# The last channel chunk of a causal convolution: from diagonal products on TensorE to scaled rows on ScalarE and sums on GpSimd

## The chip, the cores and the metric

The kernel runs on one NeuronCore of one Trainium2 chip. Five engines run their own instruction streams and meet only at semaphores: TensorE (PE; its weight loads are PEld), VectorE (DVE), ScalarE (ACT), GpSimd (POOL) and SyncE (SP), which issues nearly all DMAs. The metric is the time of one execution on the device, in microseconds (us), lower is better. The time of a kernel is the median of its runs.

## The reference, cut to what matters

Two transformer blocks follow each other. The change lies in the first one, for 512 tokens of width 1024: a projection feeds a sliding-window attention and a depthwise causal convolution of width 31 over 512 channels, and both results go through one output product. Everything is float32.

```python
def conformer_conv(u, conv_dw, conv_dw_b, conv_ln_g, conv_ln_b, w_conv_pw):
    a, gate = jnp.split(u, 2, axis=-1)
    h = a * jax.nn.sigmoid(gate)
    h = lax.conv_general_dilated(h, conv_dw[:, None, :], window_strides=(1,),
        padding=[(CONV_WIDTH - 1, 0)], feature_group_count=D_CONV, ...) + conv_dw_b
    h = jax.nn.silu(layer_norm(h, conv_ln_g, conv_ln_b))
    return h @ w_conv_pw

def sliding_window_attention(q, k, v, attn_sinks, rel_bias):
    # blocks of 128 queries; each sees its own and the previous 128 keys
    s = einsum(qb, kb) * scale + bias[bucket]          # masked outside the band
    m = max(max(s), sink); p = exp(s - m)
    p = p / (sum(p) + exp(sink - m))
    return einsum(p, vb)

hn = rms_norm(h, mix_pre_g); proj = hn @ w_in
mixed = concatenate([attn_out, conv_out], -1) @ w_out
h = h + rms_norm(mixed, mix_post_g)
```

Then come a gated feed-forward layer and the second block (another attention with a top-k choice of keys, and a mixture over 16384 experts). They are the same in both kernels.

## The kernel before

**Tiling.** The convolution holds channels on the 128 partitions, in four chunks c = 0 to 3 (CC = 4), and tokens along the row (T = 512). `hpad[:, c, :]` is a chunk's gated input with 30 zeros ahead of it. One tap w of a chunk is `cacc += taps[w] * hpad[:, c, w:w+512]`, a 128x512 scalar_tensor_tensor on VectorE (line 1786) that reads two tiles of SBUF. 31 taps make a chunk. Attention works in four blocks b of 128 queries, with 8 heads.

**Weights.** Every large product runs in three float32r passes (high and low halves), so a weight unit goes through three steps: SyncE loads it into `wraw` (three buffers), ScalarE rounds it into `WH` (line 1191, `cast_to`), and the low half `WL` is a subtraction of two SBUF tiles, on GpSimd (line 1140) or, for units 4 to 13 (`BESIDE_TAPS`) and a few others, on VectorE (line 2297). Units 8 to 13 are the keys, the values and the four query tiles; units 14 and 15 are the first of the output product.

**Order.** All orders are written out by hand, one program per engine, and nothing reorders them. VectorE goes through the taps of chunks 0, 1 and 2, with a `low` of a unit at every sixth tap; the second half of chunk 2's taps (16) is spread over the four attention blocks. On ScalarE the projections' results are copied out in the order keys, vT, q0, v, q1, q2, q3. Ahead of each copy stands `cast_to` of a unit two ahead. Each of these waits in order: an instruction that waits holds all that stand behind it.

**Chunk 3 is computed differently.** ScalarE makes diagonal matrices `tap_diag` (identity times tap, 128x128, line 1292), a few behind each copy, by `diags_plan`. TensorE multiplies them with the shifted rows of `hpad` and sums the 31 products in PSUM, in four groups `("cv", g)` (line 657), one group at the head of each attention block. VectorE adds a group's sum into `cacc[:, 3]` (lines 1852 and 1855).

**Attention.** PE: scores (line 624), transposes of the probabilities (line 636), weighted values (line 645). DVE: `logits(b)` (scale and bias, maximum; lines 1821 to 1829), `normalise(b)` (1835 to 1838), four taps of chunk 2, the group's sum, and `low(b-1)`, the low half of the block's output (1845), which frees a PSUM bank. ACT: exponentials (1302), diagonals, copies of the transposed probabilities (1311), the block's output (1315). PSUM has eight banks, taken in turn: the tile that takes a bank waits until the one eight places earlier is read. For block 1's last transpose that one is block 0's output, which `low(0)` frees.

**After attention** `conv_tail` takes the mean over the four chunks (line 682), for which every chunk must be done, and then the output product begins.

## Time and profile before

| | us |
|---|---|
| median of 3 runs | 2167.96 |
| lowest and highest run | 2166.16, 2172.48 |
| span of the profiled execution (first to last instruction) | 2161.6 |
| from the gated input of chunk 3 to the first scores | 81.75 to 104.11 |
| attention stage: first scores to the mean of the convolution | 104.11 to 165.55 |

The stage that the change touches is the short stretch from 76 to 170 us of the span. The rest of the kernel is bound by TensorE. Times in the rows count from the span's start. In a timeline row the first number is the start, the second how long the instruction (or the xN merged ones) took, and in brackets stands the idle time of the engine before it and what ended it. "took" includes the time in which an instruction has been started but can't proceed. The median of the runs is 6.4 us above the profiled span; the profiled execution has no other time of its own.

### The profile page before, as it was taken

Reading aid. Unit: us, or ns where it says so; the run is one execution under the profiler, and the core shown is the slowest. Engines: PE = TensorE matmul, PEld = TensorE weight load, DVE = VectorE, ACT = ScalarE, POOL = GpSimd, SP = SyncE. Lnnn points to the kernel's source line nnn. Section 1 sums busy time; section 2 is a strip of 40 time slices with the busy share of each in tenths; the row PEclk is TensorE's granted clock in tenths of the full one; section 3 lists DMA queues with packets and bytes.
Section 4 is the critical chain, followed back from the end, with each engine's and each line's share of the span. In section 5 each row is a group of like instructions: output and inputs, shape, how many; then the busy total and the mean of one; then the engine's idle time right before and its main releaser. Section 6 shows DMA issues by size and latency. Waiting matters only on the chain.

```text
span 2161.6 us, 29125 instructions
## 1 busy us (share of the span) xinstructions
PE 2121.7 (98%) x10648; PEld 1837.8 (85%) x10648; DVE 1442.4 (67%) x2713; ACT 858.3 (40%) x1306; POOL 1038.6 (48%) x573
## 2 busy tenths in 40 slices
PE   8989999999999999999999999999999999999999
PEld 7857888888877877899999999999998888888887
DVE  5973411110054995369998777787867999999987
ACT  4354522232264454253334444444433333333332
POOL 1203244443423333435566888888863444444342
PEclk9999999999999999999999999999999999999999
DMA  4202344444442222334347899998899999999996
GB/s 177 82 27 62 104 117 127 117 119 115 117 118 74 86 71 77 117 106 121 112 147 207 242 267 321 284 315 249 261 309 318 388 388 371 373 375 377 369 359 251
DMA packets 240489, 444.14 MB, mean 205 GB/s; under 512 B 102459, under 2 KB 152028, under 8 KB 240220
## 3 DMA queue, kind: packets, MB, share of 16 engines
q1 hardware_dynamic: 152060, 299.07, 41.8%
q0 software_dynamic: 55488, 134.83, 19.3%
q10 hardware_dynamic: 32800, 8.39, 1.8%
q8 instruction: 85, 1.39, 0.3%
q14 instruction: 56, 0.46, 0.1%
HBM read 397.71 MB, written 44.50 MB: 205 GB/s over the span
## 4 chain that ended last, share of the span: by engine, by line
PE 69%; POOL 13%; DVE 8%; issue 4%; DMA 3%; ACT 2%; SPq 0%; DVEq 0%; ACTq 0%; POOLq 0%
PE bank L469 22%; PE bank L473 22%; PE bank L472 22%; POOL gate_matrices L1151 9%; POOL y L1160 4%; DMA y<-in_peer_u_rows,gidx 3%; DVE m L1979 1%; PE bank L923 1%; DVE xn L1980 1%; DVE WL L2297 1%; PE bank L645 1%; DMA wraw<-in_peer_u 1%; ACT sc L1302 1%; DVE y L2308 0%; DVE hots L2329 0%
## 5 line engine op out<-in xcount | busy, mean ns | idle before, releaser
L1140 POOL TENSOR_TENSOR WL<-wraw,WH 128x1024 fp32r<-128x1024 f32 x171 | 435.9, 2552 | 723.5 <-ACT WH L1191 723.5
L1191 ACT ACTIVATE WH<-wraw 128x1024 fp32r<-128x1024 f32 x411 | 435.0, 1060 | 627.4 <-PE bank L469 393.6
L469 PE MATMUL bank<-XH,WH 128*128 128x384 f32 (+2 forms) x1864 | 668.8, 359 | 12.6 <-DVE WL L2297 7.8
L473 PE MATMUL bank<-XH,WL 128*128 128x384 f32 (+2 forms) x1864 | 657.8, 353 | 0.0
L472 PE MATMUL bank<-XL,WH 128*128 128x384 f32 (+2 forms) x1864 | 657.6, 353 | 0.0
L469 PEld LDWEIGHTS bank<-XH,WH 128*128 128x128 f32 x1864 | 351.4, 189 | 46.3 <-issue 12.9
L472 PEld LDWEIGHTS bank<-XL,WH 128*128 128x128 f32 x1864 | 351.6, 189 | 29.0 <-issue 0.7
L473 PEld LDWEIGHTS bank<-XH,WL 128*128 128x128 f32 x1864 | 351.1, 188 | 28.7
L2297 DVE TENSOR_TENSOR WL<-wraw,WH 128x1024 fp32r<-128x1024 f32 x240 | 293.0, 1222 | 57.6 <-ACT WH L1191 51.8
L469 PE MATMUL bank<-WH,GH 128*128 128x512 f32 x768 | 298.9, 389 | 1.6 <-issue 1.6
L473 PE MATMUL bank<-WH,GL 128*128 128x512 f32 x768 | 298.8, 389 | 0.0
L472 PE MATMUL bank<-WL,GH 128*128 128x512 f32 x768 | 298.8, 389 | 0.0
L1160 POOL DMA_INDIRECT y<-in_peer_v,gidx x128 | 185.2, 1447 | 220.7 <-DVE hN L2316 203.0
L1151 POOL DMA_INDIRECT gate_matrices<-scat_gate,scat_at x128 | 243.7, 1904 | 40.9 <-issue 38.4
L2308 DVE CUSTOM_DVE_ANT_0 y<-y,x_nat 128x1024 f32<-128x1024 f32 x128 | 156.0, 1223 | 108.6 <-DMA y<-in_peer_u_rows,gidx 103.4
L1160 POOL DMA_INDIRECT y<-in_peer_u_rows,gidx x128 | 169.3, 1323 | 106.1 <-DVE gdot L2308 77.0
L469 PEld LDWEIGHTS bank<-WH,GH 128*128 128x128 f32 x768 | 144.1, 188 | 32.3 <-issue 2.3
L473 PEld LDWEIGHTS bank<-WH,GL 128*128 128x128 f32 x768 | 144.1, 188 | 29.9
L472 PEld LDWEIGHTS bank<-WL,GH 128*128 128x128 f32 x768 | 144.2, 188 | 29.8
L2316 DVE SCALAR_TENSOR_TENSOR hN<-y,gdot,hN 128x1024 f32<-128x1024 f32 x128 | 163.9, 1280 | 3.6 <-DMA y<-in_peer_v,gidx 0.6
L1589 ACT ACTIVATE ac<-bank 128x384 f32<-128x384 f32 x122 | 59.8, 490 | 239.0 <-PE bank L473 223.6
L1904 DVE TENSOR_TENSOR y<-bank,y 128x512 f32<-128x512 f32 x22 | 15.2, 692 | 208.2 <-PE bank L473 208.2
(313 smaller groups left out, 2561.8 us busy)
## 6 DMA issues: line engine op xcount, KB each, us to landing
wraw<-in_peer_u SPq DMA_DIRECT2D x128, 512.0 KB
wraw<-in_peer_v SPq DMA_DIRECT2D x128, 512.0 KB
activations<-ac SPq DMA_DIRECT2D x122, 192.0 KB
ar<-activations SPq DMA_DIRECT2D x122, 192.0 KB
gr<-gate_matrices SPq DMA_DIRECT2D x124, 128.0 KB
wraw<-in_w_gate SPq DMA_DIRECT2D x22, 512.0 KB
wraw<-in_w_up SPq DMA_DIRECT2D x22, 512.0 KB
wraw<-in_w_down SPq DMA_DIRECT2D x22, 512.0 KB
```

Source lines behind the costliest of these rows:

```text
L469: mm = pe.matmul(out, wh, xh, start=first, stop=False)
L472: pe.matmul(out, wh, xl, start=False, stop=False)
L473: return pe.matmul(out, wl, xh, start=False, stop=last)
L645: mm = pe.matmul(out[half, (h % 4) * P:(h % 4 + 1) * P], v1[:, b - 1 + kt, half], pT1[:, h, kt, :], start=kt == kts[0], stop=kt == 1)
L1140: pool.tensor_tensor(WL[:, u % NW, 0:m], wraw[:, u % NR, 0:m], WH[:, u % NW, 0:m].bitcast(F32), ALU.subtract).then_inc(s("w_lo"), 1)
L1151: pool.indirect_dma_start(out=gate_cells[:, :], out_offset=bass.IndirectOffsetOnAxis(ap=scat_at[:, k:k + 1], axis=0), in_=scat_gate[:, k:k ...
L1160: pool.indirect_dma_start(out=gathered[:, row % NGATHER, :], out_offset=None, in_=(u_rows if row < HS else v_rows)[:, :], in_offset=bass.I ...
L1191: act.activation(WH[:, u % NW, 0:k * n], wraw[:, u % NR, 0:k * n], ACT.Copy).then_inc(s("w_hi"), 1)
L1589: act.activation(ac[:, x % NAC, :] if x < SENT else kept[:, x - SENT, :], src[:, 0:TD], ACT.Gelu_apprx_tanh).then_inc(frees(("a", x)), 1)
L2297: dve.tensor_tensor(WL[:, u % NW, 0:k * n], wraw[:, u % NR, 0:k * n], WH[:, u % NW, 0:k * n].bitcast(F32), ALU.subtract).then_inc(made, 1)
L2308: dve.tensor_tensor_reduce(out=at, in0=at, in1=x_nat[:, :], scale=1.0, scalar=0.0, op0=ALU.mult, op1=ALU.add, accum_out=gdot[:, row:row + ...
L2316: dve.scalar_tensor_tensor(out=hN[:, NTD, :], in0=at, scalar=gdot[:, row - HS:row - HS + 1], in1=hN[:, NTD, :], op0=ALU.mult, op1=ALU.add) ...
```

## The change

Chunk 3's taps leave TensorE and PSUM. ScalarE writes `taps[w] * hpad[:, 3, w:w+512]` (128x512) into one of four slots `tap_scaled`, the bias going into the first. GpSimd adds the products up in `cacc[:, 3]`, 30 additions of 128x512, each waiting for the product (`tap_scaled`) and for the addition before (`tap_added`). The product w waits for addition w-4, whose slot it takes (and for the first addition, where w is 4 or 5). `scaled_plan` says how many products follow each copy: 0, 4, 4, 0, 4, 4, 4 in the projections, and 6 and 5 in attention blocks 0 and 1.

Four orders change with it:

- GpSimd does all the additions ahead of the low half of unit 14.
- VectorE makes the gated input of chunk 3 some six taps earlier and has no group sums.
- TensorE has no group of tap products at a block's head, and `scores(b + 2)` now stands behind `weighted_values(b)`.
- ScalarE does the exponentials of block b+1 ahead of the products and copies of block b.

The first place is ScalarE, from the cast of unit 11 to the copy of q1. `WH` is a cast, `xn` and `cln` are the tiles that hold diagonals or products. Before:

```order
L1191 ACTIVATE WH<-wraw 128x1024
L1280 ACTIVATE vT<-bank 128x512
L1292 ACTIVATE xn<-ident,taps 128x128 x3
L1191 ACTIVATE WH<-wraw 128x1024
L1280 ACTIVATE q<-bank 128x512
L1292 ACTIVATE xn<-ident,taps 128x128 x2
L1191 ACTIVATE WH<-wraw 128x1024
L1280 ACTIVATE v<-bank 128x512
L1292 ACTIVATE cln<-ident,taps 128x128 x2
L1280 ACTIVATE q<-bank 128x512
```

After:

```order
L1189 ACTIVATE WH<-wraw 128x1024
L1278 ACTIVATE vT<-bank 128x512
L1291 ACTIVATE xn<-hpad,vec,taps 128x512
L1291 ACTIVATE xn<-hpad,taps 128x512
L1291 ACTIVATE cln<-hpad,taps 128x512 x2
L1189 ACTIVATE WH<-wraw 128x1024
L1278 ACTIVATE q<-bank 128x512
L1291 ACTIVATE xn<-hpad,taps 128x512 x2
L1291 ACTIVATE cln<-hpad,taps 128x512 x2
L1189 ACTIVATE WH<-wraw 128x1024
L1278 ACTIVATE v<-bank 128x512
L1278 ACTIVATE q<-bank 128x512
```

Behind the copies of vT and of each q there now stand four 128x512 products in place of two or three 128x128 diagonals; the casts keep their places behind them, and from the fifth product on each waits for GpSimd.

The second place is TensorE at the head of attention: `kk,q` are scores (the row of 128x128 is block 0, the next ones blocks 1 and 2), `hpad,xn` and `hpad,cln` tap products, `ident,sc` transposes, `pT,v` weighted values. Before:

```order
L624 MATMUL bank<-kk,q 128x128 x8
L624 MATMUL bank<-kk,q 128x256 x8
L657 MATMUL bank<-hpad,xn 128x512 x8
L624 MATMUL bank<-kk,q 128x256 x8
L636 MATMUL bank<-ident,sc 128x128 x8
L645 MATMUL bank<-pT,v 64x128 x8
L657 MATMUL bank<-hpad,cln 128x512 x8
```

After:

```order
L623 MATMUL bank<-kk,q 128x128 x8
L623 MATMUL bank<-kk,q 128x256 x8
L635 MATMUL bank<-ident,sc 128x128 x8
L644 MATMUL bank<-pT,v 64x128 x8
L623 MATMUL bank<-kk,q 128x256 x8
L635 MATMUL bank<-ident,sc 128x128 x16
L644 MATMUL bank<-pT,v 64x128 x16
```

The tap products are gone, and block 2's scores moved from ahead of block 0's transposes to behind its weighted values.

```diff
--- before.py
+++ after.py
@@ -307,9 +307,8 @@
             oneh = sb("oneh", [BUCKETS + 1, SKEW], F32, sc)
             cln = sb("cln", [P, 2, T], F32, sc)
 
-        tap_diag = [tile[:, a, m * P:(m + 1) * P] for tile in (xn, cln) for a in range(2) for m in range(4)]
-        diags_plan = [3, 3, 2, 2, 2, 2, 2, 8, 7]
-        TAP_GROUPS = [(0, 8), (8, 16), (16, 24), (24, TAPS)]
+        tap_scaled = [tile[:, a, :] for tile in (xn, cln) for a in range(2)]
+        scaled_plan = [0, 4, 4, 0, 4, 4, 4, 6, 5]
         brow = sc1[:, :, :, :].rearrange("p a h n -> p (a h n)")[:, 0:NH * SKEW].rearrange("p (h n) -> p h n", h=NH)
         skew_dram = nc.dram_tensor("skew_rows", (P, NH, SKEW), F32).ap()
 
@@ -646,26 +645,13 @@
                                        pT1[:, h, kt, :], start=kt == kts[0], stop=kt == 1)
                 full(mm, "o", b)
 
-            def last_chunk_taps(g):
-
-                w0, w1 = TAP_GROUPS[g]
-                out = take("cv", g)
-                for w in range(w0, w1):
-                    pe.wait_ge(s("diags_made"), w + 1)
-                    if w == 0:
-                        wait_read(pe, ("ca", CC - 1))
-                    mm = pe.matmul(out[:, :], tap_diag[w % len(tap_diag)], hpad[:, CC - 1, w:w + T], start=w == w0,
-                                   stop=w == w1 - 1)
-                full(mm, "cv", g)
-
             def attention():
                 scores(0)
                 scores(1)
                 for b in range(NT):
-                    last_chunk_taps(b)
+                    weighted_values(b)
                     if b + 2 < NT:
                         scores(b + 2)
-                    weighted_values(b)
 
             def mixed(i):
 
@@ -678,7 +664,7 @@
                     if c < CC - 1:
                         pe.wait_ge(s("conv_done"), c + 1)
                     else:
-                        wait_read(pe, ("cv", NT - 1))
+                        pe.wait_ge(s("tap_added"), TAPS - 1)
                     mm = pe.matmul(out[:, :], ones[:, :], cacc[:, c, :], start=c == 0, stop=c == CC - 1)
                 full(mm, "cmean", 0)
                 for b in range(NT):
@@ -1063,7 +1049,7 @@
                 if u == unit_at[("ci", 0)] + 2:
                     second_inputs()
                 if u == unit_at[("wo", 0, 2)]:
-                    wait_full(sp, ("cv", NT - 1))
+                    sp.wait_ge(s("tap_added"), TAPS - 1)
                     sp.dma_start(gain_row, A["mix_post_row"].partition_broadcast(P)).then_inc(s("post_row_landed"), 16)
                 if u >= unit_at[("wg", 4)] and (u - unit_at[("wg", 4)]) % 4 == 0 and u < unit_at[("wg", 4)] + 4 * (NEXP // ZBLOCKS):
                     if u == unit_at[("wg", 4)]:
@@ -1122,9 +1108,21 @@
                       allow_small_or_imprecise_dtypes=True).then_inc(s("own_row_made"), 1)
             pool.memset(zeros[:, :], 0.0).then_inc(s("zeros_made"), 1)
 
+            def last_chunk():
+
+                at = cacc[:, CC - 1, :]
+                for w in range(1, TAPS):
+                    pool.wait_ge(s("tap_scaled"), w + 1)
+                    if w > 1:
+                        pool.wait_ge(s("tap_added"), w - 1)
+                    pool.tensor_tensor(at, tap_scaled[0] if w == 1 else at, tap_scaled[w % len(tap_scaled)],
+                                       ALU.add).then_inc(s("tap_added"), 1)
+
             for u, (k, n, _) in enumerate(units[:LOW_BY_DVE]):
                 if u in BESIDE_TAPS or u in NORM_LOWS:
                     continue
+                if u == BESIDE_TAPS.stop:
+                    last_chunk()
                 if u == unit_at[("u2", 1)]:
                     pool.wait_ge(s("wsr_landed"), 16)
                     pool.affine_select(out=wsr[:, :, :], in_=wsr[:, :, :], compare_op=ALU.is_ge, fill=0.0, base=0,
@@ -1278,23 +1276,25 @@
                     cast_to(("v", 0) if key == ("vT", 0) else ("q", 1) if key == ("v", 0) else key)
                     src = wait_full(act, key)
                     act.activation(dst, src[:, :], ACT.Copy).then_inc(frees(key), 1)
-                    last_chunk_diags()
-
-            diags, stages = [0], iter(diags_plan)
-
-            def last_chunk_diags():
-
-                for w in range(diags[0], diags[0] + next(stages, 0)):
-                    if w >= len(tap_diag):
-                        g = next(n for n, (w0, w1) in enumerate(TAP_GROUPS) if w0 <= w - len(tap_diag) < w1)
-                        wait_full(act, ("cv", g))
-                    at = w * CC + CC - 1
-                    act.activation(tap_diag[w % len(tap_diag)], ident[:, :], ACT.Copy,
-                                   scale=taps[:, at:at + 1]).then_inc(s("diags_made"), 1)
-                    diags[0] = w + 1
+                    last_chunk_products()
+
+            scaled, stages = [0], iter(scaled_plan)
+
+            def last_chunk_products():
+
+                c = CC - 1
+                for w in range(scaled[0], scaled[0] + next(stages, 0)):
+                    if w == 0:
+                        wait_read(act, ("ca", c))
+                    if w >= len(tap_scaled):
+                        act.wait_ge(s("tap_added"), max(w - len(tap_scaled), 1))
+                    act.activation(tap_scaled[w % len(tap_scaled)], hpad[:, c, w:w + T], ACT.Identity,
+                                   scale=taps[:, w * CC + c:w * CC + c + 1],
+                                   bias=vcol("dw_b", c) if w == 0 else 0.0).then_inc(s("tap_scaled"), 1)
+                    scaled[0] = w + 1
 
             def attention():
-                for b in range(NT):
+                def exps(b):
                     w = P if b == 0 else 2 * P
                     st = st1[:, b % 2]
                     act.wait_ge(s("sink_gap"), b + 1)
@@ -1302,7 +1302,12 @@
                         act.activation(sc1[:, b % 2, h, 0:w], sc1[:, b % 2, h, 0:w], ACT.Exp, bias=st[:, 1, h:h + 1],
                                        accum_out=st[:, 2, h:h + 1])
                     act.activation(st[:, 4, :], st[:, 3, :], ACT.Exp).then_inc(s("exps"), 1)
-                    last_chunk_diags()
+
+                exps(0)
+                for b in range(NT):
+                    if b + 1 < NT:
+                        exps(b + 1)
+                    last_chunk_products()
                     for i in range(NH // 2):
                         src = wait_full(act, ("pT", b, i))
                         kt0 = 1 if b == 0 else 0
@@ -1799,7 +1804,7 @@
                         tap(c, w)
                         if w - alone < alone:
                             tap(c + 1, w - alone)
-                        if c == CC - 3 and w == alone:
+                        if c == 0 and w == TAPS - 3:
                             gated(CC - 1)
                 for u in beside:
                     low(u, s("w_beside"))
@@ -1845,16 +1850,6 @@
                     dve.tensor_tensor(XL[:, 0:4, to], src[:, :].rearrange("p (c q) -> p c q", c=4),
                                       XH[:, 0:4, to].bitcast(F32), ALU.subtract).then_inc(frees(("o", b)), 1)
 
-                def last_chunk(g):
-                    src = wait_full(dve, ("cv", g))
-                    at = cacc[:, CC - 1, :]
-                    if g == 0:
-                        done = dve.tensor_scalar(at, src[:, :], vcol("dw_b", CC - 1), None, ALU.add)
-                    else:
-                        wait_read(dve, ("cv", g - 1))
-                        done = dve.tensor_tensor(at, at, src[:, :], ALU.add)
-                    done.then_inc(frees(("cv", g)), 1)
-
                 logits(0)
                 for b in range(NT):
                     if b + 1 < NT:
@@ -1862,7 +1857,6 @@
                     normalise(b)
                     for w in taps_left[b * len(taps_left) // NT:(b + 1) * len(taps_left) // NT]:
                         tap(w)
-                    last_chunk(b)
                     if b:
                         low(b - 1)
                 low(NT - 1)
```

## Rows read from the trace of the kernel before

**Rows 1.** The page: busy shares, and shares of the chain of waits.
```profile
PE 2121.7 (98%) x10648; PEld 1837.8 (85%) x10648; DVE 1442.4 (67%) x2713; ACT 858.3 (40%) x1306; POOL 1038.6 (48%) x573
PE 69%; POOL 13%; DVE 8%; issue 4%; DMA 3%; ACT 2%; SPq 0%; DVEq 0%; ACTq 0%; POOLq 0%
```

**Rows 2.** Windows: PE, PEld, DVE, ACT, POOL busy us (count), PEclk, DMA share, GB/s.
```profile
76.00:104.00 28.00, 27.23 (x122) 22.20 (x121) 27.89 (x41) 12.61 (x27) 9.41 (x1) 1.00 0.23 75
104.11:165.55 61.44, 55.12 (x294) 35.41 (x294) 44.12 (x65) 30.91 (x105) 4.34 (x2) 0.97 0.08 26
```

**Rows 3.** Timeline, VectorE, end of the convolution: no row has idle time before it.
```profile
81.75 0.68 DVE L1770 TENSOR_TENSOR hpad<-bank,sg 128x512 f32<-128x512 f32 x1
82.35 3.40 DVE L1786 SCALAR_TENSOR_TENSOR cacc<-hpad,taps,cacc 128x512 f32<-128x512 f32 x5
...
86.80 4.06 DVE L1786 SCALAR_TENSOR_TENSOR cacc<-hpad,taps,cacc 128x512 f32<-128x512 f32 x6
90.77 1.22 DVE L2297 TENSOR_TENSOR WL<-wraw,WH 128x1024 fp32r<-128x1024 f32 x1
91.91 12.01 DVE L1786 SCALAR_TENSOR_TENSOR cacc<-hpad,taps,cacc 128x512 f32<-128x512 f32 x18
```

**Rows 4.** Timeline, GpSimd: its low half of unit 14, beside that chain.
```profile
94.59 11.54 POOL L1140 TENSOR_TENSOR WL<-wraw,WH 128x1024 fp32r<-128x1024 f32 x1 [63.86 <-ACT WH L1191]
```

**Rows 5.** Groups by form, GpSimd, whole span: busy us, mean ns of one.
```profile
L1140 POOL TENSOR_TENSOR WL<-wraw,WH 128x1024 fp32r<-128x1024 f32 x170 | 434.6, 2559 | 723.5 <-ACT WH L1191 723.5
...
L1140 POOL TENSOR_TENSOR WL<-wraw,WH 128x544 fp32r<-128x544 f32 x1 | 1.4, 1358 | 0.0
```

**Rows 6.** Timeline, ScalarE: the last cast and copy of the projections.
```profile
98.90 1.05 ACT L1191 ACTIVATE WH<-wraw 128x1024 fp32r<-128x1024 f32 x1
103.26 0.60 ACT L1280 ACTIVATE q<-bank 128x512 f32<-128x512 f32 x1 [3.31 <-PE bank L473]
```

**Rows 7.** Timeline, VectorE, first block of attention.
```profile
105.38 1.29 DVE L1821 SCALAR_TENSOR_TENSOR sc<-bank,biasT 128x512 f32<-128x512 f32 x2 [1.46 <-PE bank L624]
...
107.96 0.51 DVE L1827 TENSOR_TENSOR st<-st,sinkb 128x8 f32<-128x8 f32 x1
...
108.66 2.48 DVE L1821 SCALAR_TENSOR_TENSOR sc<-bank,biasT 128x512 f32<-128x512 f32 x4
111.17 2.29 DVE L1826 TENSOR_REDUCE st<-sc 128x8 f32<-128x2048 f32 x1
...
115.42 3.11 DVE L1786 SCALAR_TENSOR_TENSOR cacc<-hpad,taps,cacc 128x512 f32<-128x512 f32 x4
```

**Rows 8.** Timeline, a later stage: a GpSimd pass, and VectorE's third of four rows.
```profile
634.55 2.43 POOL L1140 TENSOR_TENSOR WL<-wraw,WH 128x1024 fp32r<-128x1024 f32 x1 [3.83 <-ACT WH L1191]
634.63 2.63 DVE L1949 SCALAR_TENSOR_TENSOR ck<-ck,st,gkv 128x256 f32<-128x256 f32 x1
```

**Rows 9.** Windows, the tap products' matmuls (line 657) alone in the attention stage.
```profile
104.11:165.55 61.44, 28.16 (x62) 11.61 (x62) 0.97 0.08 26
```

**Rows 10.** Groups by form, 76 to 190 us: ScalarE and VectorE in attention.
```profile
L1302 ACT ACTIVATE sc<-sc,st 128x256 f32<-128x256 f32 x24 | 11.8, 495 | 0.0
...
L1838 DVE TENSOR_TENSOR sc<-sc,st 128x2048 f32<-128x2048 f32 x3 | 6.9, 2291 | 0.1
...
L1311 ACT ACTIVATE pT<-bank 128x512 f32<-128x512 f32 x12 | 6.3, 601 | 8.6 <-PE bank L636 8.6
...
L1202 ACT ACTIVATE sq<-cacc 128x512 f32<-128x512 f32 x4 | 2.5, 631 | 5.7 <-DVE cacc L1875 4.5 <-PE bank L502 1.2
```

**Rows 11.** Timeline, TensorE: weighted values of blocks 0 and 1.
```profile
120.55 2.71 PE L645 MATMUL bank<-pT,v 128*64 128x128 f32 x16 [0.86 <-DVE sc L1821]
...
136.90 3.33 PE L645 MATMUL bank<-pT,v 128*64 128x128 f32 x32 [0.86 <-DVE sc L1821]
```

**Rows 12.** Windows ahead of and over block 0's weighted values (columns as in rows 2).
```profile
118.00:120.80 2.80, 0.69 (x4) 0.46 (x5) 2.19 (x4) 0.38 (x1) 0.00 (x0) 0.99 0.00 0
120.80:124.20 3.40, 3.40 (x18) 2.56 (x17) 3.37 (x4) 0.91 (x3) 0.00 (x0) 0.50 0.02 7
```

## The prediction, made before the changed kernel was run

> **What bounds the kernel now.** I read first the page, then windows over the two stages that the change touches, then the timelines of each engine in them, last the groups for durations. The page shows TensorE busy for 98% of the span and as most of the chain of waits [rows 1]. That is a mean, and it hides the stretch at issue. From 76 to 104 us VectorE is busy for 27.9 of 28 us, TensorE for 27.2, and ScalarE and GpSimd have room [rows 2]; TensorE sets the pace there, with VectorE close behind. From the first scores at 104.1 to the mean of the convolution at 165.55, which is 61.4 us, no engine is full: TensorE 55.1, VectorE 44.1, ScalarE 30.9 [rows 2]. Half of TensorE's part are the tap products, 28.2 us in 62 passes [rows 9]. The chain goes logits, maximum, exponentials, normalise, transposes, copies, weighted values, and the tap products lie mostly beside the exponentials. So their 28 us are not for the taking.
>
> **What the change adds.** ScalarE: 31 products of 128x512. A square of that shape takes 0.63 us [rows 10]; back to back I take 0.54, since a cast of twice the width takes 1.05 [rows 6]. GpSimd: 30 additions of 128x512 with two SBUF operands. It has 2.56 us for 1024 columns and 1.36 for 544 [rows 5], so 1.28 for 512 by the slope. Bounds are 1.0 and 1.4; with the wait on its own last result I take 1.31, thus 39 us in one serial chain.
>
> **The step that decides: two engines, one way into SBUF.** GpSimd's low half of unit 14 started at 94.59 and took 11.54 us, where 2.56 is usual [rows 4, 5]. Beside it VectorE ran taps without a gap until 103.9 [rows 3]; 103.9 + 2.2 is 106.1, the end of GpSimd's row. So GpSimd did nothing while the taps ran, though it had asked for 13 boundaries between them. The other way round, a 128x8 operation took 0.51 us while GpSimd's second pass was under way [rows 7]. The new additions read two SBUF tiles as that pass did, and stand beside the same taps.
>
> The Trainium skill, page "SBUF — State Buffer", part "Who interferes with whom", says that a VectorE instruction with two SBUF inputs and a GpSimd instruction that reads SBUF exclude each other for a whole instruction, and that whichever issues first goes first. The exclusion agrees with [rows 4]. First come, first served does not, since GpSimd then had its turn at 95.3; a later place agrees with it [rows 8]. That reading is the first rival below.
>
> **Projections, step by step.** The gated input of chunk 3 is written some 5 us earlier than at 81.75 [rows 3], which costs VectorE nothing. Products 0 to 3 come behind the copy of vT (81.0), so the first addition can start at 82.7. VectorE has then begun its gapless row. ScalarE goes on to the copy of q0 and blocks at product 4 (87.0), which waits for addition 1. Behind it in ScalarE's queue stands the cast of unit 13, for whose low half VectorE comes by at 90.8 [rows 3]. VectorE stops there, and that frees the way. Additions 1 to 3 end at 92.2, 93.5 and 94.8; product 7 and the cast follow until 96.3; VectorE, behind addition 5, does the low half from 97.4 to 98.5. TensorE wants unit 13 at 97.8, one copy of 5.4 us ahead of 103.26 [rows 6], so it loses 0.8.
>
> VectorE now has its 18 last taps, 12.0 us [rows 3], and shuts GpSimd out until 110.5. ScalarE blocks at product 10, which waits for addition 6. Behind it stand the copies of q2 and q3. Product 15, the last ahead of the copy of q3, waits for addition 11. Additions 6 to 11 take 6 x 1.31 = 7.9, until 118.4; the product, a cast (0.95) and the copy (0.60) give the first scores at 120.5 in place of 104.1: **+16.4 us**. Who waits is TensorE, with nothing else to do.
>
> **Attention, step by step, at full clock.** Scores at 120.5. Logits 0 took 3.3 us [rows 7] and now wait twice behind an addition, 2.4: 126.4. Logits 1 are 2.5 + 2.3 and 0.3 of small ones [rows 7]: 131.5. ScalarE has exponentials 1 (8 x 0.49 [rows 10]) until 135.7 and then six products, of which the last waits for addition 21. Additions 20 and 21 wait for VectorE's normalise and four taps (3.1 [rows 7]) and end at 139.0. The copies of transposed probabilities stand behind that, so block 0's values end at 141.6, and only then come scores 2: 21.1 us for this block. Block 1: logits 2 until 147.4, normalise (2.3 [rows 10] and 0.3) until 150.0, four taps and the low half, which frees a bank for the last transpose, until 153.8. ScalarE meanwhile has exponentials 2 and five products until 154.9. Four copies at 0.5 [rows 10] and the values (3.3 [rows 11]) bring scores 3 at 158.9: 17.3. Block 2: logits, normalise, taps, low half, last transpose, values: 175.1, 16.2. Block 3 needs only transposes and values, its exponentials having been made ahead: 180.3, 5.3. The sum is 59.9 against 61.4: **-1.5**. What the missing 28 us of tap products give, the later scores take back: logits(b + 2) can't start before block b is through. VectorE's four group sums (0.7 each) count in this. The last addition is at 159, well ahead of the mean, and the low half of unit 14 at 162 is early enough; the loads of units 17 and 18, which wait for low halves, come 50 us later than before and are still first needed past 185.
>
> **The clock.** After 2.8 us with TensorE busy for 0.69 the granted clock was 0.50 for 3.4 us [rows 12], the lower level of 1.2 GHz against 2.4. Block 0's 16 passes took 2.71 us there, 0.169 each, against 32 in 3.33, 0.104 each, at full clock [rows 11]: 1.6 times. In the new order TensorE idles for 16 us ahead of the first scores and for some 6 us in each block. On the path it carries about 13 us of transposes, values and scores in the sum above. At 0.6 of that, all at half clock, the price is 8; the other bound is nothing. I take 7, since the drop shown came after a far shorter pause: **+7**.
>
> Sum: +16.4 - 1.5 + 7 = 21.9. The profiled span of 2161.6 becomes 2183.5. The median of the runs is 6.4 above the span, so I forecast **2190 us**. With additions of 1.0 us it is 3 less, with 1.4 it is 2 more, and the clock gives 2182 to 2191.
>
> **Rivals.** *The two engines take turns (20%).* At one place GpSimd asked while a VectorE instruction ran, and the next one, though started without a gap, took 2.63 us behind it [rows 8]. Then from 82.7 on VectorE's 21 us of work in the convolution and about 19 additions of 1.31 share the way, and logits 0 start near 129 instead of 105.4 (+24); attention, with fewer additions left, gives back 3; the clock adds 7: 2196. Against it stand the same instructions at the same place [rows 4].
>
> *They hardly disturb each other (17%).* If ScalarE's products came early enough and additions slipped in beside taps, scores would start at 104.1, and attention without waits behind additions would take about 57 us: -4, or 2164 at full clock; with spells of half clock 2164 to 2172. It needs that the 9 us of standstill [rows 4] be something else than VectorE's taps. I split it into 11% faster and 6% the same. 0.3%, or 6.5 us, is about what a measurement of this kernel can tell from no change.
>
> *The standstill is real but shorter (10%).* VectorE stops once more, or the copies of q2 and q3 get ahead: half of the 16.4, so +8 to +14: 2176 to 2182. *No change in effect* is no case: every engine's order differs.
>
> **How the numbers follow.** The forecast has 50%, taking turns 20%, the shorter standstill 10%, no disturbance 17%, and 3% something slower still. Slower by over 0.3% is thus 83%, faster 11%, the same 6%. The range reaches from 2172, which leaves out the faster rival, to 2204, which takes in taking turns with the longest additions.
>
> **What the new profile would show.** Right: additions on GpSimd of many microseconds beside the taps, the first at about 83 that ends past 91 and one of over 10 us that ends past 110; the first scores at 118 to 123; TensorE idle ahead of them; the low clock in attention; 58 to 68 us from the scores to the mean. Wrong in the main step: additions of 1.3 us all along and scores near 104, or taps that each take 2 us. Wrong in the second: an attention stage under 55 us. The stretch behind 190 us of the span should be the same, only shifted.

## The result, and the profile after

The changed kernel takes 2185.41 us (median of 4 runs, 2182.96 to 2188.93) against 2167.82 us for the kernel before (4 runs beside it). The ratio is 1.0076 with a 95% interval of 1.0054 to 1.0097: slower by 17.6 us. The prediction said 2190 and a range of 2172 to 2204. The size came out near; the way to it did not, and that is what the runs are about.

The profiled execution has a span of 2181.0 us against 2161.6. Its busy shares and its chain of waits, as in [rows 1]:

```profile
PE 2105.0 (97%) x10586; PEld 1836.0 (84%) x10586; DVE 1457.4 (67%) x2709; ACT 866.3 (40%) x1306; POOL 1077.8 (49%) x603
PE 76%; DVE 9%; POOL 7%; DMA 3%; issue 3%; ACT 2%; SPq 0%; DVEq 0%; ACTq 0%; POOLq 0%
```

TensorE has 62 matmuls fewer, and VectorE is busy for 15 us longer with four instructions fewer. Something makes VectorE's instructions longer. Since executions differ by some us ahead of the change already (a spell of half clock that comes early or late), I count all stages from ScalarE's copy of vT. It started at 81.02 in the trace of before and at 78.02 here.

| us, from the copy of vT | before | after |
|---|---|---|
| to the first scores | 23.09 | 33.56 |
| first scores to first logits | 1.27 | 5.62 |
| first logits to the mean of the convolution | 60.17 | 63.82 |
| sum: copy of vT to the mean | 84.53 | 103.00 |
| from the mean to the end | 1996.1 | 2000.0 |

The sum says where the time went: 18.5 us between the copy of vT and the mean, nearly all of the difference. What lies behind the mean varied between 1991.7 and 2011.6 us over the profiled executions of all kernels here, though its instructions are the same, and nothing is read from that.

VectorE in the projections, where [rows 3] had five taps in 3.40 us, six in 4.06 and eighteen in 12.01 (timeline: start, us, engine, line, operation, output<-inputs, count):

```profile
80.13 8.61 DVE L1791 SCALAR_TENSOR_TENSOR cacc<-hpad,taps,cacc 128x512 f32<-128x512 f32 x5
88.66 2.30 DVE L2291 TENSOR_TENSOR WL<-wraw,WH 128x1024 fp32r<-128x1024 f32 x1
90.88 10.22 DVE L1791 SCALAR_TENSOR_TENSOR cacc<-hpad,taps,cacc 128x512 f32<-128x512 f32 x6
101.02 2.28 DVE L2291 TENSOR_TENSOR WL<-wraw,WH 128x1024 fp32r<-128x1024 f32 x1
103.22 14.05 DVE L1791 SCALAR_TENSOR_TENSOR cacc<-hpad,taps,cacc 128x512 f32<-128x512 f32 x18
```

And GpSimd beside it, the additions of the new sum:

```profile
80.00 1.36 POOL L1118 TENSOR_TENSOR cacc<-xn 128x512 f32<-128x512 f32 x1 [48.98 <-ACT xn L1291]
81.50 3.27 POOL L1118 TENSOR_TENSOR cacc<-cacc,cln 128x512 f32<-128x512 f32 x2
...
102.36 3.76 POOL L1118 TENSOR_TENSOR cacc<-cacc,cln 128x512 f32<-128x512 f32 x2
112.01 7.79 POOL L1118 TENSOR_TENSOR cacc<-cacc,xn 128x512 f32<-128x512 f32 x2 [5.89 <-ACT xn L1291]
```

Six taps in 10.22 us are 1.70 each, where 0.67 was usual. Two additions in 3.27 (with the 0.14 between them) are 1.56 each. One pair, a tap and an addition, takes 1.70 us: 0.4 of the tap's and 1.3 of the addition's. So the two engines take turns, one instruction each, from 80 us until the fifteenth addition ends at 106.1. Then GpSimd has no product for 5.9 us, and its sixteenth addition, asked for at 112.01, is held up for 5 us until VectorE's last tap is over at 117.3. That one row looks like [rows 4]; the fifteen ahead of it look like [rows 8].

What TensorE and ScalarE make of it (in brackets the idle time ahead, and what ended it):

```profile
91.10 0.47 PE L468 MATMUL bank<-XH,WH 128*128 128x512 f32 x1 [1.75 <-DVE WL L2291]
103.44 0.77 PE L468 MATMUL bank<-XH,WH 128*128 128x512 f32 x1 [6.63 <-DVE WL L2291]
```

```profile
104.31 1.06 ACT L1189 ACTIVATE WH<-wraw 128x1024 fp32r<-128x1024 f32 x1 [4.42 <-PE bank L468]
110.73 0.60 ACT L1278 ACTIVATE q<-bank 128x512 f32<-128x512 f32 x1 [5.36 <-PE bank L472]
```

TensorE waits 1.75 and 6.63 us for VectorE's low halves of two weight units, which stand behind eleven slow taps; the rest of the 10.5 us is the product for q3, part of it at half clock. ScalarE's products are not what anybody waits for: they find an addition missing once in this stretch, for 0.33 us.

In attention TensorE's rows read like this (compare block 0's values in [rows 11], 2.71 and 3.33, and the clock in [rows 12]):

```profile
111.57 3.41 PE L623 MATMUL bank<-kk,q 64*128 64x128 f32 x32 [0.88 <-ACT q L1278]
128.12 1.97 PE L635 MATMUL bank<-ident,sc 128*128 128x128 f32 x8 [13.13 <-DVE sc L1843]
135.20 2.85 PE L644 MATMUL bank<-pT,v 128*64 128x128 f32 x16 [5.12 <-ACT pT L1316]
137.98 3.46 PE L623 MATMUL bank<-kk,q 64*128 64x256 f32 x16
148.17 2.82 PE L635 MATMUL bank<-ident,sc 128*128 128x128 f32 x12 [6.73 <-DVE sc L1843]
...
156.66 2.10 PE L623 MATMUL bank<-kk,q 64*128 64x256 f32 x16
165.79 2.82 PE L635 MATMUL bank<-ident,sc 128*128 128x128 f32 x12 [7.04 <-DVE sc L1843]
...
170.46 5.47 PE L644 MATMUL bank<-pT,v 128*64 128x128 f32 x32
```

And VectorE's logits of blocks 2 and 3, with the time it stood idle for the scores that now come late:

```profile
140.09 2.58 DVE L1826 SCALAR_TENSOR_TENSOR sc<-bank,biasT 128x512 f32<-128x512 f32 x4 [9.01 <-PE bank L623]
...
157.82 2.48 DVE L1826 SCALAR_TENSOR_TENSOR sc<-bank,biasT 128x512 f32<-128x512 f32 x4 [5.07 <-PE bank L623]
```

Three things can hide in these 18.5 us: additions in the way of VectorE, scores that come after the values instead of ahead, and TensorE at half clock. The windows over both stages show the last (busy us and count of PE, PEld, DVE, ACT, POOL, then PEclk):

```profile
94.00:104.00 10.00, 3.37 (x14) 2.50 (x13) 10.00 (x7) 3.04 (x5) 9.28 (x6) 0.79 0.00 0
111.57:181.02 69.45, 34.81 (x233) 30.50 (x233) 48.95 (x70) 35.17 (x103) 28.99 (x17) 0.68 0.07 24
```

### The profile page after: what moved, and what is told of

It reads as the page before. It is cut to its first block, busy times and chain, and to the rows that moved or that the text cites. A ratio compares the mean times of both kernels' runs of the same rounds, so it can differ in the third digit from the quotient of the medians.

```text
span 2181.0 us, 29049 instructions
## 1 busy us (share of the span) xinstructions
PE 2105.0 (97%) x10586; PEld 1836.0 (84%) x10586; DVE 1457.4 (67%) x2709; ACT 866.3 (40%) x1306; POOL 1077.8 (49%) x603
## 4 chain that ended last, share of the span: by engine, by line
PE 76%; DVE 9%; POOL 7%; DMA 3%; issue 3%; ACT 2%; SPq 0%; DVEq 0%; ACTq 0%; POOLq 0%
PE bank L468 24%; PE bank L472 24%; PE bank L471 23%; POOL gate_matrices L1149 5%; DVE cacc L1791 2%; POOL y L1158 2%; PE bank L937 1%; DMA y<-in_peer_u_rows,gidx 1%; DVE m L1973 1%; PE bank L644 1%; DMA wraw<-in_peer_u 1%; PE bank L909 1%; DVE WL L2291 1%; DVE xn L1974 1%; DVE sc L1826 0%
## 5 line engine op out<-in xcount | busy, mean ns | idle before, releaser
L1138 POOL TENSOR_TENSOR WL<-wraw,WH 128x1024 fp32r<-128x1024 f32 x171 | 425.5, 2491 | 624.6 <-ACT WH L1189 624.6
L1898 DVE TENSOR_TENSOR y<-bank,y 128x512 f32<-128x512 f32 x22 | 15.2, 692 | 208.2 <-PE bank L472 208.2
```

Source lines behind the costliest of these rows:

```text
L1138: pool.tensor_tensor(WL[:, u % NW, 0:m], wraw[:, u % NR, 0:m], WH[:, u % NW, 0:m].bitcast(F32), ALU.subtract).then_inc(s("w_lo"), 1)
```

## The experiments

In the kernels' names below, "early scores" means that TensorE makes the scores of block b+2 ahead of the values of block b. Stage times are from one profiled execution each. The stage from the copy of vT to the first scores came out between 23.08 and 23.10 us in seven kernels, so a stage can be read to about 0.1 us where nothing disturbs it. Where additions disturb it, it can't. Four of the kernels are the same up to the first scores (the change, early scores, the fill at one addition, fillers on TensorE), and their stage took 33.56, 33.07, 33.06 and 31.92 us. The run with the fill is nearly a second execution of the whole changed kernel, and it has 100.5 us from the copy of vT to the mean where the first had 103.0. So differences against the 103.0 are good to some 2.5 us, not to tenths.

### Additions that read nothing

```diff
-                    pool.tensor_tensor(at, tap_scaled[0] if w == 1 else at, tap_scaled[w % len(tap_scaled)],
-                                       ALU.add).then_inc(s("tap_added"), 1)
+                    pool.memset(at, 0.0).then_inc(s("tap_filled"), 1)
+                    pool.wait_ge(s("tap_filled"), w)
+                    pool.memset(at, 0.5).then_inc(s("tap_added"), 1)
```

> The changed kernel with each of GpSimd's 30 additions replaced by two fills of the accumulator, which write SBUF and read none of it; the sum of the last chunk is left out. Theory (VectorE's taps and GpSimd's additions exclude each other because both read SBUF): the taps from 80 us on take 0.7 to 0.8 us each and stand without gaps as in the kernel before, and from the copy of vT to the first scores it takes 23 to 25 us (23.1 before, 33.6 after). Rival (ScalarE's products, each of which waits for an addition, and the copies queued behind them cost the time, whatever the additions do): 30 us or more at fills of the same length, and taps of 0.75 us with TensorE waiting for ScalarE's copies. Rival (any GpSimd work on SBUF disturbs, writes too): taps of 1.5 us or more again.

Timeline of VectorE and of GpSimd:

```profile
92.07 12.01 DVE L1792 SCALAR_TENSOR_TENSOR cacc<-hpad,taps,cacc 128x512 f32<-128x512 f32 x18
```

```profile
93.65 0.53 POOL L1118 MEMSET cacc<- 128x512 f32 x1
94.23 0.53 POOL L1120 MEMSET cacc<- 128x512 f32 x1
```

The taps are back at 12.01 us for eighteen, to the hundredth what [rows 3] had, and vT to scores takes 23.10. From vT to the mean it takes 85.3 us, against 103.0. A pair of fills has 1.23 us from start to start and is chained as the additions were (1.41 in the undisturbed pairs), so the chain of products and waits was still there, nearly as long. GpSimd that only writes leaves the taps as they are; GpSimd *reading* SBUF costs 17.7 us, or 15.2 against the 100.5 of the second execution. The rival, that ScalarE blocks behind its products, falls.

### Additions of half the length

```diff
+                    if w == 1:
+                        pool.memset(at, 0.0).then_inc(s("acc_zeroed"), 1)
+                        pool.wait_ge(s("acc_zeroed"), 1)
-                    pool.tensor_tensor(at, tap_scaled[0] if w == 1 else at, tap_scaled[w % len(tap_scaled)],
+                    pool.tensor_tensor(at[:, 0:T // 2], tap_scaled[0][:, 0:T // 2] if w == 1 else at[:, 0:T // 2],
...
```

> The changed kernel with each addition over 256 of the 512 columns (the other half of the last chunk's sum is left out, the accumulator is cleared first). Theory (turns: each tap waits for one addition): additions of 0.65 to 0.75 us in place of 1.3, taps at a spacing of 1.2 to 1.3 us in place of 1.8, from the copy of vT to the first scores 27 to 30 us (33.6 after), and the attention stage 2 to 4 us shorter than 69.5. Rival (starvation behind the gapless taps sets the time): unchanged within 2 us, since the wait doesn't depend on how long an addition is. Rival (the additions are off the path in attention): attention stays at 69.5 within 1 us.

```profile
88.72 6.48 DVE L1794 SCALAR_TENSOR_TENSOR cacc<-hpad,taps,cacc 128x512 f32<-128x512 f32 x6
95.13 1.76 DVE L2294 TENSOR_TENSOR WL<-wraw,WH 128x1024 fp32r<-128x1024 f32 x1
```

Additions took 0.73 us alone, and a disturbed tap 1.21 to 1.23: the turns hold. But the stage to the first scores went all the way back, 23.09, where 27 to 30 were expected. Six taps in 6.48 us let the low half end at 96.9, and TensorE wants it at about 97.9. The delay is no sum of slow taps; it is what is left of it beyond VectorE's reserve ahead of a low half. What the additions still cost shows one step later, 9.3 us from the first scores to the first logits, since VectorE must finish its taps first. The attention stage came to 70.4, no shorter than 69.5, as the second rival had it; from the first logits it is 61.2 against 63.8.

### Products and additions in attention only

```diff
-        scaled_plan = [0, 4, 4, 0, 4, 4, 4, 6, 5]
+        scaled_plan = [0, 0, 0, 0, 0, 0, 0, 9, 9, 8, 5]
```

> The changed kernel with no products and additions during the projections: the stages of ScalarE make 9, 9, 8 and 5 products in the four blocks of attention. Theory: vT copy to first scores back at 23 to 24 us (33.6 after), no long TensorE pause ahead of them; the additions (39 us in a chain) then stand beside logits and normalise, so attention takes 72 to 85 us against 69.5. Rival (the delay ahead of the scores has to do with the earlier gated input or VectorE's order, not with additions): still 30 us or more to the scores.

To the scores 23.09, as the theory had it, and 84.6 us of attention: 107.7 to the mean, slower than the change itself; 2198.8 us in its one run. The earlier gated input and the new order of VectorE are thereby cleared of the delay ahead of the scores. The place is worse, since nine products stand in one row ahead of ScalarE's copies, each waiting for an addition.

### Scores ahead of values

```diff
                 for b in range(NT):
-                    weighted_values(b)
                     if b + 2 < NT:
                         scores(b + 2)
+                    weighted_values(b)
```

> The changed kernel with TensorE's scores of block b+2 ahead of the weighted values of block b, as far ahead as in the kernel before. Theory (the new order of scores costs part of the attention stage, since logits b+2 can start only once block b is through): from first scores to the mean 60 to 66 us against 69.5, VectorE's pauses of 9.0 and 5.1 us ahead of logits 2 and 3 gone, whole time 4 to 9 us less than the changed kernel. Rival (the order is no limit, GpSimd's additions and the half clock are): 68 to 71 us, within 2 us of the changed kernel.

The attention stage takes 59.1 us against 69.4, and vT to the mean 92.2 against 103.0: 10.8 us. The time is 2177.0 us, ratio to before 1.0033 (1.0011 to 1.0054), so 1.0076 minus this is 0.43%, or 9.3 us. VectorE's idle 9.0 and 5.1 us ahead of logits 2 and 3 are gone (0 and 0.8 now). The order that the change takes for granted is a cost of its own. Part of it may come by way of the clock: TensorE is at half clock for 30.7 us of this attention stage against 44.4, so the price of the order and the price of the clock below may overlap and can't simply be added.

### Both causes out

The two edits together (fills, and early scores).

> The changed kernel with both causes taken away at once: fills of the accumulator in place of GpSimd's additions (the sum of the last chunk is left out) and TensorE's scores of block b+2 ahead of the values of block b. If the two costs are separate and add up (17.7 us for the additions by the first run, 10.8 us for the order of the scores, both counted from the copy of vT to the mean of the convolution, 103.0 in the changed kernel), this stretch takes 74 to 77 us, against 84.5 in the kernel before; then what the change could give at best, with nothing in its way, is 8 to 10 us. If they hide one another, it takes 79 to 86 us.

vT to the mean takes 72.9 us, 1.1 below the expected 74 to 77: within what one execution can tell, the costs are separate and add up (17.7 + 10.8 = 28.5; 30.1 measured). Against the 84.5 of before this is the worth of the idea with nothing in its way: 11.6 us, since 28 us of tap products on TensorE [rows 9] lie mostly beside other work.

### A fill at one addition

```diff
+            scratch = sb("scratch", [P, 192], F32, sc)
...
+                    if w == 17:
+                        pool.memset(scratch[:, :], 0.0)
```

> The changed kernel with one short fill of a scratch tile on GpSimd ahead of the seventeenth addition alone, so that this addition asks for SBUF some 0.2 to 0.35 us later within a tap of VectorE. In three traces an addition or a low half that asked 0.03 to 0.12 us into a tap that follows another without a gap was held up until the whole row of taps was over (6.4 to 11.5 us for 1.3 or 2.4); in six places one that asked 0.14 to 0.49 us into a tap had the next turn. If the moment of asking decides: the seventeenth addition takes 1.3 to 2.0 us, and the last taps stand at 1.8 us each behind it in place of 0.66. If instead the state of the two engines decides (a first request after a pause meets a row of taps): over 5 us again, whatever the moment.

GpSimd around the fill:

```profile
112.79 6.53 POOL L1121 TENSOR_TENSOR cacc<-cacc,xn 128x512 f32<-128x512 f32 x1 [5.09 <-ACT xn L1294]
119.44 0.26 POOL L1120 MEMSET scratch<- 128x192 f32 x1
119.66 1.26 POOL L1121 TENSOR_TENSOR cacc<-cacc,xn 128x512 f32<-128x512 f32 x1
```

The addition that is held up is the sixteenth (w = 16), and the fill stands ahead of the seventeenth. So the fill came behind the wait and moved nothing, and the question of the expectation was not put to the chip. What the run gives is a second execution of the change. Its sixteenth addition asked at 112.79, 0.65 us into a tap where the change had 0.12, and was held up again, for 6.53 us in all. The last section comes back to the moment of asking.

### Work for TensorE in its pauses

```diff
+            def filler(b):
+                out = take("fill", b)
+                for i in range(8):
+                    mm = pe.matmul(out[:, :], ident[:, :], hpad[:, CC - 1, i:i + T], start=True, stop=True)
...
                 for b in range(NT):
+                    filler(b)
                     weighted_values(b)
```

> The changed kernel with 8 more products on TensorE at the head of each block of attention, of constant and padded input into a bank that nobody reads, so that TensorE is busy where it stood idle; the result is the same. Theory (TensorE's pauses bring it to half clock for 23.9 us and 13.7 us, and that costs part of the stage): the spells at half clock in attention shrink below half of their 44 us, and the stage (69.5 us) shortens by 2 to 5 us if the new products lie in the pauses. Rival (half clock costs nothing there, since TensorE waits for others anyway, or the new products, some 7 us a block, come into the way): unchanged or up to 8 us longer.

2194.36 us, ratio 1.0116 (1.0075 to 1.0156): 82.6 us of attention, 13 more, though the half clock in it fell from 44.4 us to 27.3. Of the 13 us, 6.0 lie ahead of the first logits, and what made them began ahead of the first filler (115.25): here the sixteenth addition, asked for at 112.34, was not held up, four more additions took turns with taps, and the logits stand behind these taps. The other 7.1 lie behind. Each filler took 7.1 us, and the later ones stood at the head of a block, where the values and the next scores stood behind it. This says nothing on the clock, only that such work must fit into the pause.

### Exponentials ahead, alone, in the kernel before

This is the kernel before with this one part of the change. In block 0 the diagonals stay ahead of the exponentials of block 1.

```diff
-                for b in range(NT):
+                def exps(b):
...
-                    last_chunk_diags()
+                exps(0)
+                for b in range(NT):
+                    if b == 0:
+                        last_chunk_diags()
+                    if b + 1 < NT:
+                        exps(b + 1)
+                    if b:
+                        last_chunk_diags()
```

> The kernel before (tap products on TensorE from diagonals, no additions on GpSimd) with one part of the change alone: ScalarE makes the exponentials of block b+1 ahead of block b's copies of transposed probabilities. If that part is worth something by itself: attention 57 to 60 us against 61.4, 2163 to 2166 us. If it costs, since block b's transposes and diagonals stand behind 4 us of exponentials: 63 to 66 us, up to 2173. If others set the pace: within 1 us.

2162.68 us (12 runs) against 2168.73, ratio 0.9973 (0.9949 to 0.9997). Attention takes 60.1 us against 61.4. This part of the change was worth having by itself: 1.3 us by the stage, and between 0.7 and 11 us by the interval of the medians, which can't say it closer. In before the transposes of blocks 2 and 3 waited 0.41 and 1.27 us for normalised probabilities, and here neither waits (no bracket in the rows):

```profile
145.14 1.91 PE L636 MATMUL bank<-ident,sc 128*128 128x128 f32 x16
146.98 3.33 PE L645 MATMUL bank<-pT,v 128*64 128x128 f32 x32
150.24 6.28 PE L657 MATMUL bank<-hpad,cln 128*128 128x512 f32 x14
156.35 1.91 PE L636 MATMUL bank<-ident,sc 128*128 128x128 f32 x16
```

### Running sums in PSUM: the way out

In all traces VectorE's logits, which read a bank and an SBUF tile, ran at 0.68 us beside additions, while taps and `normalise`, with two SBUF inputs, waited. So the taps' second input was moved. TensorE claims two banks ahead of the product of vT and marks them with one small matmul each; VectorE keeps the running sums of chunks 1 and 2 there, and writes to `cacc` with the last tap ahead of attention.

```diff
+                for c in (2, 1):
+                    out = take("acc", c)
+                    full(pe.matmul(out[:, 0:P], ident[:, :], ident[:, :], start=True, stop=True), "acc", c)
                 tile(("v", 0), ("vT", 0))
...
+                    held = {1: range(alone, TAPS - 1), 2: range(0, alone - 1)}.get(c, ())
+                    into = read = cacc[:, c, :]
...
+                    if w in held:
+                        into = bank_of(("acc", c))[:, :]
+                    if w - 1 in held:
+                        read = bank_of(("acc", c))[:, :]
...
-                    done = dve.scalar_tensor_tensor(out=cacc[:, c, :], in0=hpad[:, c, w:w + T],
+                    done = dve.scalar_tensor_tensor(out=into, in0=hpad[:, c, w:w + T],
                                                     scalar=taps[:, w * CC + c:w * CC + c + 1],
-                                                    in1=cacc[:, c, :], op0=ALU.mult, op1=ALU.add)
+                                                    in1=read, op0=ALU.mult, op1=ALU.add)
```

> The changed kernel with the scores of block b+2 ahead of the values of block b, and with VectorE's running sums of chunks 1 and 2 kept in two PSUM banks until attention begins, so that a tap reads one SBUF tile (the padded input) and one bank instead of two SBUF tiles; GpSimd's additions stay as they are. The traces so far say that logits, which read a bank and an SBUF tile, run at 0.68 us beside additions, and that taps, normalise and small operations with two SBUF inputs wait for them. Theory (it is the second SBUF input that makes VectorE and GpSimd exclude each other): taps at 0.66 to 0.75 us beside additions of 1.27 us, from the copy of vT to the first scores 23 to 24.5 us (33.1 with this order of scores and sums in SBUF), from there to the mean 50 to 57 us, whole time 2148 to 2158 us, faster than both kernels. Rival (any read of SBUF by both excludes): taps at 1.8 us again and 2170 to 2180 us.

VectorE, and GpSimd beside it:

```profile
87.37 4.04 DVE L1805 SCALAR_TENSOR_TENSOR bank<-hpad,taps,bank 128x512 f32<-128x512 f32 x6
91.32 1.26 DVE L2307 TENSOR_TENSOR WL<-wraw,WH 128x1024 fp32r<-128x1024 f32 x1
92.51 10.62 DVE L1805 SCALAR_TENSOR_TENSOR bank<-hpad,taps,bank 128x512 f32<-128x512 f32 x16
```

```profile
91.64 3.54 POOL L1121 TENSOR_TENSOR cacc<-cacc,cln 128x512 f32<-128x512 f32 x2
95.33 2.73 POOL L1121 TENSOR_TENSOR cacc<-cacc,xn 128x512 f32<-128x512 f32 x2
98.20 2.77 POOL L1121 TENSOR_TENSOR cacc<-cacc,cln 128x512 f32<-128x512 f32 x2
```

Six taps in 4.04 us where the change had 10.22, sixteen in 10.62 (0.66 each), and two additions in 2.73 at the same time. Ahead of attention only the low halves, which still read two SBUF tiles, hold a pair of additions up (3.54). vT to scores is 23.09, vT to the mean 77.9. The time is 2160.45 us (11 runs) against 2171.11: ratio 0.9959 (0.9945 to 0.9974). This beats the kernel before by 0.4% and the changed kernel by 1.2%. The median lies a little above the 2148 to 2158 expected; the profiled execution, 2153.0, was the fastest of its eleven.

### The same sums with late scores

> The changed kernel, scores in its own order, with the running sums of chunks 1 and 2 in banks alone. Theory: vT copy to first scores 23.1 us as with both edits; the late scores cost their part again, so that from the copy of vT to the mean it takes 86 to 90 us (77.9 with both edits, 92.2 with the early scores alone, 103.0 in the changed kernel). If the late scores cost nothing once the way into SBUF is free: 78 to 80 us.

vT to the mean takes 88.6 us, inside the expected 86 to 90. The stage to the first scores takes 23.70 us, not the 23.1 expected, and so it does in the next version. TensorE's row says why:

```profile
102.94 3.45 PE L626 MATMUL bank<-kk,q 64*128 64x128 f32 x32 [1.49 <-DVE cacc L1805]
```

The scores wait for the last tap that reads a running sum, since it is this tap that frees the bank. In the version with both edits it was over just in time (23.09), so the sums in PSUM have a small price of their own, 0.6 us in two executions of three.

With that there are four corners:

| us, copy of vT to the mean | late scores | early scores |
|---|---|---|
| running sums in SBUF | 103.0 (the change) | 92.2 |
| running sums in PSUM | 88.6 | 77.9 |

Down a column it is 14.4 and 14.3 us for the second SBUF input of these taps, along a row 10.8 and 10.7 for the late scores. That the two agree to 0.1 us is in part luck: with the second execution of the change, 100.5, it would be 11.9 down and 8.3 along. They are separate costs of some 12 to 14 and 8 to 11 us. The additions cost more than that, 15.2 to 17.7 by the fills. The remainder of some 3 us would lie in instructions that the sums in PSUM leave as they are (low halves, `normalise`, the taps in attention); it was not taken apart.

### The clock, in the version that is left

```diff
                 scores(0)
                 scores(1)
+                out = take("fill", 0)
+                for i in range(6):
+                    mm = pe.matmul(out[:, :], ident[:, :], hpad[:, CC - 1, i:i + T], start=True, stop=True)
...
```

> The version with running sums in banks and early scores, with 6 more products on TensorE behind the scores of block 1 (constant by padded input, into a bank that nobody reads), so that TensorE is busy for some 5 of the 6.9 us in which it waited ahead of the first transposes. Theory (the pause brings TensorE to half clock, and the passes on the path behind it then take 1.6 times as long): the spell of 13.7 us at half clock behind that pause is gone, block 0's eight transposes take 1.1 to 1.3 us in place of 1.97 and its values 1.7 to 1.9 in place of 2.85, and the stage from first scores to mean is 1 to 3 us shorter than 54.8. Rival: the clock falls all the same, or the passes were hidden: the stage within 0.5 us, or longer by as much as the new products come late.

TensorE in the version without and with it:

```profile
116.62 1.97 PE L638 MATMUL bank<-ident,sc 128*128 128x128 f32 x8 [6.91 <-DVE sc L1859]
123.72 2.85 PE L647 MATMUL bank<-pT,v 128*64 128x128 f32 x16 [5.13 <-ACT pT L1319]
...
130.41 1.53 PE L638 MATMUL bank<-ident,sc 128*128 128x128 f32 x12 [1.36 <-DVE sc L1859]
```

```profile
104.99 5.42 PE L656 MATMUL bank<-hpad,ident 128*128 128x512 f32 x12
110.34 2.10 PE L626 MATMUL bank<-kk,q 64*128 64x256 f32 x16
112.86 1.09 PE L638 MATMUL bank<-ident,sc 128*128 128x128 f32 x8 [0.42 <-DVE sc L1865]
119.96 2.85 PE L647 MATMUL bank<-pT,v 128*64 128x128 f32 x16 [6.00 <-ACT pT L1325]
```

The same eight transposes take 1.09 us behind a busy TensorE and 1.97 behind a pause of 6.9. The values stay at 2.85, since a second pause of 6.0 us stands ahead of them, which the filler doesn't reach. (The third row of the first fence is block 1's twelve transposes at full clock.) The stage shortens by 1.4 us, 54.8 to 53.4, so this half of the expectation holds. In the time of the kernel it doesn't show: ratio to before 0.9980 (0.9962 to 0.9999), no better than 0.9959 without it.

## Why the prediction was right, and where not

**What bounds the kernel: right.** The attention stage gave no 28 us: with both obstacles gone it gave 11.6.

**The step that decides: wrong.** "GpSimd did nothing while the taps ran" was read from one row [rows 4] and carried over to all additions: the copies of q2 and q3 would stand behind products that wait for starved additions. What happened is the first rival, turns of one instruction each. The single row was real, and it happened once again (112.01, 7.79 us for two), but it is the exception, and [rows 8] was the rule. One premise was off as well: the first addition was taken to find VectorE already in its gapless row of taps, and it asked at 80.00, just ahead of the first of them at 80.13. The chain of reasoning behind it (ScalarE blocks at product 4, then at 10, then the copy of q3) is void: no product waited over 0.33 us. Who waited is right, TensorE; for whom is wrong: for VectorE's low halves (8.4 us), not for ScalarE.

**Its price: near by luck.** +16.4 us were forecast ahead of the first scores. It was 10.5 to the scores and 4.3 from there to the first logits, 14.8 together. The rival's own working gave +24 there: it had 19 additions of 1.31 us added to VectorE's row. In fact fifteen took turns; then GpSimd had no product for 5.9 us and after that was held up, so that VectorE's last sixteen taps ran free, eight ahead of the request and eight during it.

**Attention at full clock, -1.5: size wrong, mechanism right.** First scores to mean is 69.4 us, first logits to mean 63.8, against 60.2. Take from 69.4 the 8.1 us of half clock below and it is about 61.3 in place of 59.9. That the later scores take back what the missing products give was right: the run with early scores puts it at 10.8 us. With the scores early the stage is shorter than before, 59.1 us against 61.4. The prediction named this, and missed that it could be had back by swapping two lines.

**The clock, +7: borne out by the rows, tested in part.** The rows give it piece by piece: eight transposes 1.97 for 1.09, twice twelve 2.82 for 1.53, the values of block 2 5.47 for 3.33, the scores of block 2 3.46 for 2.10, and block 0's values 2.85 for 1.67 (16 at 0.104, [rows 11]). Together 8.1 us, if each lies on the path. Only the first pause was tested, and filling it gave 1.4.

**"They hardly disturb each other": what it asks for.** This rival gave 2164 to 2172. The version that removes the disturbance in the projections and keeps the rest of the change (sums in PSUM, late scores) had 2168.7 in its one run.

**The sum.** +21.9 was forecast for the span, and the profiled one came out at +19.4, of which 18.5 lie in the stage; the medians differ by 17.6. Two steps were off, in opposite ways. Split at the first scores, as the forecast was, it is +10.5 where +16.4 was said, and +8.0 where +5.5 was said for attention with its clock. The two errors, of 5.9 and 2.5 us, cancelled in part. The 6.4 us added for the median was large too: it is 4.4 here.

## What to carry to other kernels

Before work is given to GpSimd, list what VectorE runs beside it, and count each VectorE instruction with two SBUF inputs as longer by one GpSimd instruction that reads SBUF; where one of its inputs could live in PSUM, or GpSimd only wrote, that cost was gone here. A wait that appears far from the change may be an order that came along with it (here scores behind values, 8 to 11 us): try the order by itself before judging the idea. One starved row in a trace tells what can happen, and the many short rows beside it what usually does: count both kinds before pricing a chain by either.

## What the runs showed of the hardware

**Which instructions exclude each other.** With an addition or a low half on GpSimd, these VectorE instructions waited: taps (1.70 us each for 0.66), low halves (2.30 for 1.22), the products of `normalise` (3.27 for 2.29). These did not: logits, from a bank and an SBUF tile (four in 2.48), taps with their sum in a bank (six in 4.04), maxima (2.29), and anything beside GpSimd's fills. The Trainium skill, page "SBUF — State Buffer", part "Who interferes with whom", states that an instruction of VectorE with two SBUF inputs contends with a GpSimd instruction that reads SBUF, and not with one that only writes. The runs agree, with the numbers above.

The number of inputs is not all, though. A `tensor_scalar` has one SBUF input, and some of them waited beside an addition. Here are one from the change, of 0.17 us elsewhere, and one from the run with fillers, of 0.55 elsewhere:

```profile
119.96 1.27 DVE L1833 TENSOR_SCALAR st<-st 128x8 f32<-128x8 f32 x1
82.24 1.32 DVE L1797 TENSOR_SCALAR cacc<-hpad,taps,vec 128x512 f32<-128x512 f32 x1
```

The same part of the Trainium skill exempts an instruction with at most one SBUF input only outside VectorE's 2-port modes, and counts `tensor_scalar` among those that can enter such a mode. These two rows agree with that; no run here turned the mode on or off.

**Who is next is not settled.** Mostly the two alternate. But in five places GpSimd asked and got nothing until VectorE's row of taps was over: in before at 94.59 (11.54 us), in the version with exponentials ahead at 91.83 (12.55), and at the sixteenth addition in the changed kernel (6.38), with early scores (6.48) and with the fill (6.53). In all five VectorE's taps had run undisturbed for at least 4.6 us, and GpSimd had read nothing for at least 5. The taps were those of the projections, which start 0.66 us apart and take 0.74 each, so that one begins before the other ends. In nine other places in such rows GpSimd had paused for under 3 us, or the row was less than 1 us old, and it had the next turn.

A long pause alone is not the cause. In seven places in attention GpSimd had paused for 9.7 to 12.9 us and had the turn at once, though VectorE had run undisturbed for 4.5 us (in the change at 150.34, 1.27 us for the addition). The taps there start 0.78 us apart, with 0.04 to 0.05 us free between them. The moment within a tap is not the cause alone either: it was 0.03 to 0.65 us in the five, and at the same 0.12 us the sixteenth addition was held up in the change and had the next turn in the run with fillers, after a pause of 2.58 us. Whether the length of the undisturbed row, that of GpSimd's pause or the missing gap between taps decides was not tried. The Trainium skill's sentence at the same place, that whoever issues first gets the shared pair for the whole instruction, covers the alternation; for these five it is not enough, since seven to fifteen later taps went first.

**A reserve hides slow taps completely, and then not at all.** With additions of 0.73 us each disturbed tap took 1.22 and TensorE lost nothing ahead of the scores (23.09 us); with additions of 1.27 it lost 10.5, and between 8.8 and 10.5 over the four executions.
